# Block 2 of a two-block layer stack: selection pairs ahead of sliding pairs, window keys and values made later, latent norms in three steps

## What is computed

```
h = rmsnorm(x, mix_norm)
c_q, c_kv, k_rope, n_q, n_kc, n_vc, n_ks, n_vs, n_kw, n_vw, n_gate, sb_q, sb_k, sb_v = split(h @ w_in)
# 1. latent attention, 6 heads: softmax over all earlier tokens
q  = rmsnorm(c_q, q_norm) @ w_uq ;  k, v = rmsnorm(c_kv, kv_norm) @ w_ukv ;  rope on 32 columns
# 2. three branches that share 6 query heads (2 key heads), each with its own gate
o_cmp = softmax(q . kc) vc          # kc, vc: 31 compressed blocks, made by a small gelu MLP
o_sel = softmax(q . ks, selected blocks, causal) vs   # with 8 blocks all are selected
o_win = softmax(q . kw, sliding window 512, causal) vw
o_nsa = g0 * o_cmp + g1 * o_sel + g2 * o_win
# 3. stick-breaking attention, 4 heads
a = exp(log_sigmoid(z) + suffix sums of log_sigmoid(-z)) ;  o_sb = a v
x = x + concat(o_mla, o_nsa, o_sb) @ w_out
```

## Time and profile before

| | |
|---|---|
| median of three runs | 3490.95 us (3486.69 to 3496.64) |
| the profiled execution | 3486.4 us, span 3484.6 us |
| TensorE busy | 3376.5 us, 97% of the span |
| VectorE, ScalarE, GpSimd busy | 1652.7, 1226.2, 199.2 us |
| bytes moved | 288.19 MB |

### The profile page before, as it was taken

The page is one execution under the profiler, slowest core; times in us unless marked ns, Lnnn a source line. Parts: engine busy times, 40 slices in busy tenths (PEclk is TensorE's granted clock), DMA queues, the critical chain, the costliest instruction groups (busy, mean ns, idle before and its releaser), DMA issues.

```text
span 3484.6 us, 42143 instructions
## 1 busy us (share of the span) xinstructions
PE 3376.5 (97%) x15726; PEld 2641.3 (76%) x15726; DVE 1652.7 (47%) x2158; ACT 1226.2 (35%) x1831; POOL 199.2 (6%) x247
## 2 busy tenths in 40 slices
PE   8989999999899999999998999999999999999998
PEld 6657888775688877888775688887888776678887
DVE  6755443566444335443545554434443543654433
ACT  4343122432422234222444442234222444542233
POOL 1200000011010000000002310000000001310000
PEclk9999999999999999999999999999999999999999
DMA  6213322221243222332320143333332321033331
GB/s 167 66 43 84 97 97 96 85 79 49 61 106 99 95 92 79 96 98 96 78 64 24 30 104 96 96 97 87 96 97 100 85 73 32 16 89 96 96 96 67
DMA packets 434262, 288.19 MB, mean 83 GB/s; under 512 B 44528, under 2 KB 412316, under 8 KB 433896
## 3 DMA queue, kind: packets, MB, share of 16 engines
q1 hardware_dynamic: 431272, 280.02, 27.7%
q0 software_dynamic: 2736, 4.58, 0.9%
q10 hardware_dynamic: 144, 2.10, 0.2%
HBM read 284.53 MB, written 2.13 MB: 82 GB/s over the span
## 4 chain that ended last, share of the span: by engine, by line
PE 92%; DVE 3%; ACT 3%; issue 2%; DMA 0%; SPq 0%; DVEq 0%; ACTq 0%
PE bank L1964 27%; PE bank L1966 27%; PE bank L1965 27%; PE bank L1974 2%; PE bank L2061 1%; PE bank L2107 1%; PE bank L2083 1%; PE bank L2184 1%; PE bank L2151 1%; PE bank L2448 1%; PE bank L2450 1%; PE bank L2013 1%; PE bank L2035 0%; ACT whi L927 0%; DVE G L1506 0%
## 5 line engine op out<-in xcount | busy, mean ns | idle before, releaser
L1964 PE MATMUL bank<-hh,whi 128*128 128x512 f32 x2832 | 1140.6, 403 | 36.7 <-DVE hl L1418 22.8
L1966 PE MATMUL bank<-hh,wlo 128*128 128x512 f32 x2832 | 1107.9, 391 | 0.0
L1965 PE MATMUL bank<-hl,whi 128*128 128x512 f32 x2832 | 1107.5, 391 | 0.0
L1368 DVE TENSOR_TENSOR wlo<-raw,whi 128x1024 fp32r<-128x1024 f32 (+2 forms) x534 | 642.5, 1205 | 300.6 <-ACT whi L927 285.8
L1964 PEld LDWEIGHTS bank<-hh,whi 128*128 128x128 f32 x2832 | 535.4, 189 | 184.2 <-issue 49.4
L927 ACT ACTIVATE whi<-raw 128x1024 fp32r<-128x1024 f32 (+2 forms) x534 | 546.2, 1034 | 255.2 <-PE bank L1966 254.8
L1965 PEld LDWEIGHTS bank<-hl,whi 128*128 128x128 f32 x2832 | 535.3, 189 | 121.3 <-issue 14.2
L1966 PEld LDWEIGHTS bank<-hh,wlo 128*128 128x128 f32 x2832 | 534.5, 189 | 113.1
L1964 PE MATMUL bank<-fshi,whi 128*128 128x512 f32 (+1 forms) x1358 | 526.6, 388 | 3.5 <-DVE G L1643 2.0
L1966 PE MATMUL bank<-fshi,wlo 128*128 128x512 f32 (+1 forms) x1358 | 523.2, 385 | 0.0
L1965 PE MATMUL bank<-fslo,whi 128*128 128x512 f32 (+1 forms) x1358 | 522.8, 385 | 0.0
(11 more groups left out here) (244 smaller groups left out, 2391.6 us busy)
## 6 DMA issues: line engine op xcount, KB each, us to landing
raw<-in_ffn_w_gate SPq DMA_DIRECT2D x88, 512.0 KB, 3.8
raw<-in_ffn_w_up SPq DMA_DIRECT2D x88, 512.0 KB, 3.8
raw<-in_ffn_w_down SPq DMA_DIRECT2D x88, 512.0 KB, 3.4
raw<-in_w_in SPq DMA_DIRECT2D x78, 512.0 KB, 3.9
raw<-in_w_up SPq DMA_DIRECT2D x64, 512.0 KB, 4.0
raw<-in_w_down SPq DMA_DIRECT2D x64, 512.0 KB, 3.4
raw<-in_w_out SPq DMA_DIRECT2D x16, 512.0 KB, 4.0
raw<-in_w_in SPq DMA_DIRECT2D x18, 256.0 KB, 3.6
```

The source lines that it names most:

```text
L1368: dve.tensor_tensor(slot3(wlo, s, m), slot3(raw, s, m), slot3(whi, s, m).bitcast(F32), ALU.subtract).then_inc(c.lo_done.sem, 1)
L1964: pe.matmul(o, wh, ah, start=start, stop=False)
L1965: pe.matmul(o, wh, al, start=False, stop=False)
L1966: return pe.matmul(o, wl, ah, start=False, stop=stop)
```

## The change

It has three parts, all in block 2's mixing stage.

1. In each tile of pair entries all four sel entries come first, then the four win entries.
2. The keys and values of the win branch are made later. The full group nkw leaves `fill` and takes the place of nvwf behind `cmp_max`; the swap snkw, the full group nvwf and the transposes nvw become late groups (bank 7) and are woven with the first four pair steps. `fill` has two steps less.
3. The norm of the latents is split: `rn` is now only the sum and the reciprocal root; `rn_scale` (VectorE scaling) and `rn_split` (ScalarE high, VectorE low parts) are steps of their own, a pair step or more behind.

```diff
--- before.py
+++ after.py
@@ -197,8 +197,8 @@
     entries = []
     for t in range(NSA_PAIRS):
         entries.append(dict(kind="cmp", turn=t, t=t, new=True, done=False))
-        for i in range(QT):
-            for kind in ("sel", "win"):
+        for kind in ("sel", "win"):
+            for i in range(QT):
                 entries.append(dict(kind=kind, turn=t, t=t, i=i, n=P * (i + 1), first=False, new=False, done=kind == "win" and i == QT - 1))
     for p in range(MLA_H // 2):
         for i in range(QT):
@@ -377,8 +377,7 @@
     fill += compress(1)
     fill.append(add("gatesf", "fm", ("w_gates_pe", 0), frees="act", dst=M_POSX))
     fill += [("g", "w21"), ("g", "snks")]
-    fill.append(add("nkw", "fm", ("w_in", 1312), frees="act", dst=N_KW))
-    fill += [("g", "gates"), ("g", "snkw")]
+    fill.append(("g", "gates"))
 
     stick_steps = []
     n_stick = SB_H // 2 * QT
@@ -400,15 +399,18 @@
     steps.append(add_turned("nvs", 1184, N_TURN[0], frees="dve", dst=N_VS, off=0, pitch=128))
     steps.append(("cmp_s",))
     steps.append(("cmp_max",))
-    steps.append(add_turned("nvw", 1440, N_TURN[1], frees="dve", dst=N_VW, off=0, pitch=128))
-    steps += [("cmp_sum",), ("g", "nvs"), ("g", "nvw")]
+    steps.append(add("nkw", "fm", ("w_in", 1312), frees="act", dst=N_KW))
+    steps += [("cmp_sum",), ("g", "nvs")]
 
     late = dict(late=True)
+    groups["snkw"].update(late)
+    window = [("g", "snkw"), add_turned("nvw", 1440, N_TURN[1], frees="dve", dst=N_VW, off=0, pitch=128, **late), ("g", "nvw")]
+    groups["nvwf"].update(late)
     latent = [add(f"cq{t}", "fm", ("w_in", 128) if t else ("w_in_halves", 0), frees="act", dst=M_CQ + S * t, **late) for t in range(2)]
     latent.append(("sq", "cq"))
     latent.append(add("ckv", "fm", ("w_in", 256), frees="act", dst=M_CQ + 2 * S, **late))
-    latent += [("rn", "cq"), ("sq", "ckv")]
-    latent += [("mix", 0), ("mix", 1), ("rn", "ckv"), ("key_pe",)]
+    latent += [("rn", "cq"), ("sq", "ckv"), ("rn_scale", "cq"), ("mix", 0), ("rn_split", "cq"), ("mix", 1)]
+    latent += [("rn", "ckv"), ("key_pe",), ("rn_scale", "ckv"), ("rn_split", "ckv")]
 
     def query(h):
         if h % 3 == 0:
@@ -446,7 +448,8 @@
                 some.append(("mix", 2 + entries[k]["turn"]))
             some.append(("pair", j))
         return some
-    steps += weave(latent, run(0, O_LAG + 8))
+    steps += weave(window, run(0, QT))
+    steps += weave(latent, run(QT, O_LAG + 8))
     steps += weave(first_pair + second_pair, run(O_LAG + 8, n_nsa))
     steps += weave(third_pair, run(n_nsa, n_nsa + 6))
     steps += weave(early, run(n_nsa + 6, len(entries) + O_LAG + 1))
@@ -1279,9 +1282,11 @@
                         square(c, l, A2_KV, 0, g(M_CQ + 2 * S), narrow)
                     elif s[0] == "rn" and s[1] == "cq":
                         rms(c, l, 3, A2_Q, 2, bank[:, 7, :], 256, narrow)
+                    elif s[0] == "rn_split" and s[1] == "cq":
                         highs(c, l, 8, [fshi[:, 0, :], fshi[:, 1, :]], narrow)
                     elif s[0] == "rn":
                         rms(c, l, 4, A2_KV, 1, bank[:, 7, :], 128, narrow)
+                    elif s[0] == "rn_split":
                         highs(c, l, 10, [fshi[:, 2, :]], narrow)
                     elif s[0] == "pair":
                         pair(c, l, s[1])
@@ -1393,6 +1398,22 @@
                         dve.tensor_tensor(lo_tiles[t - 1], tmp[(t - 1) % 2], hi_tiles[t - 1].bitcast(F32), ALU.subtract).then_inc(c.rn_lo.sem, 1)
                     if beside:
                         beside(t)
+
+            def latent_scale(c, l, r, b0, at, gain, n):
+
+                _, rstd, tmp = narrow
+                dve.wait_ge(c.rn_rstd.sem, c.rn_rstd.at(l, r))
+                dve.wait_ge(c.rn_lo.sem, c.rn_lo.at(l, b0))
+                for t in range(n):
+                    dve.scalar_tensor_tensor(out=tmp[t], in0=g(at + S * t), scalar=prm[:, gain + t:gain + t + 1], in1=rstd, op0=ALU.mult,
+                                             op1=ALU.mult).then_inc(c.rn_tmp.sem, 1)
+
+            def latent_low(c, l, b0, first, n):
+
+                tmp = narrow[2]
+                for t in range(n):
+                    dve.wait_ge(c.rn_hi.sem, c.rn_hi.at(l, b0 + t + 1))
+                    dve.tensor_tensor(fslo[:, first + t, :], tmp[t], fshi[:, first + t, :].bitcast(F32), ALU.subtract).then_inc(c.rn_lo.sem, 1)
 
             def add_squares(c, l, at, t):
 
@@ -1880,10 +1901,12 @@
                         group(c, b, l, b["groups"][s[1]])
                     elif s[0] == "px":
                         blocks(c, b, l, s[1])
-                    elif s[0] == "rn" and s[1] == "cq":
-                        norm(c, l, 3, 24, [g(M_CQ), g(M_CQ + S)], prm[:, P2_QN:P2_QN + 2], [fshi[:, 0, :], fshi[:, 1, :]], [fslo[:, 0, :], fslo[:, 1, :]], narrow)
-                    elif s[0] == "rn":
-                        norm(c, l, 4, 26, [g(M_CQ + 2 * S)], prm[:, P2_KVN:P2_KVN + 1], [fshi[:, 2, :]], [fslo[:, 2, :]], narrow)
+                    elif s[0] == "rn_scale" and s[1] == "cq":
+                        latent_scale(c, l, 3, 24, M_CQ, P2_QN, 2)
+                    elif s[0] == "rn_scale":
+                        latent_scale(c, l, 4, 26, M_CQ + 2 * S, P2_KVN, 1)
+                    elif s[0] == "rn_split":
+                        latent_low(c, l, *((24, 0, 2) if s[1] == "cq" else (26, 2, 1)))
                     elif s[0] == "key_pe":
                         key_pe(c, b, l)
                     elif s[0] == "turn_q":
@@ -2043,6 +2066,8 @@
                     q, n, at, sb_ = e["q"], e["n"], P * e["i"], score_banks(e)
                     if q == 0:
                         need(c, b, l, *(gr["name"] for gr in b["order"] if gr.get("evac", True) and not gr.get("late")))
+                    if e["kind"] == "win" and e["i"] == e["t"] == 0:
+                        need(c, b, l, "snkw", "nvw")
                     if e["kind"] == "mla" and e["i"] == 0:
                         p = e["pair"]
                         need(c, b, l, f"mk{p}", *(f"mv{t}" for t in range(QT)))
```

## The result

The changed kernel takes 3504.52 us, the median of five runs (3499.69 to 3505.05), against 3486.69 us for the kernel before in the same comparison. The ratio is 1.0036, with a 95% interval of 1.0025 to 1.0048: slower. (The quotient of those two medians alone is 1.0051. The recorded ratio is smaller, and the two profiled executions side with it.) The profiled execution took 3499.69 us; its span is 3497.9 us, 13.3 us (0.38%) more than before, where 14.2 were forecast.

The account below looks back on a forecast made before the run. TensorE was taken to bound the kernel. Per layer 8.3 us (stick phase) - 2.2 (opening) + 1 (clock) = 7.1, +14.2 for two layers on 3490.95: 3505 us predicted, 8 in 10 within 3491 to 3520.

Parts of the forecast that it names:

- The new order of the fillers: Stick phase: with nkw and snkw out of `fill`, TensorE waits 12.4 us in place of 4.1, 8.3 more per layer.
- the first `sbo`: Stick phase: with c01 instead of nq2 ahead of it, it waits 4.1 us for `suf_exp 3` on ScalarE.
- `z 6`: Stick phase: waits 5.6 us for `suf_exp 4`, a 7.1 us chain with only `suf 4` and snq2 left as cover.
- The opening: Opening of the pairs: waits of 5.4 us in place of 7.6, so 2.2 us less per layer.
- The 1.4 us before nvwf: Opening: nvwf needs bank 7 and waits 1.4 us for the swap's VectorE operations, behind 0.7 of scores.
- The 1.0 before the first scores: Opening: scores of sel 0.0, without cq0 as cover, wait 1.0 us for the copy of nvs.
- The 2.7 us that I laid to `rn_scale`: Opening: VectorE's scaling delays win 0.3's scores by 0.3 us, win 0.1's transposes by 1.9, win 0.2's by 0.5.
- The clock: Stick phase and opening: lower clock behind two new waits, less one that goes, 1 us each: net +1 per layer.
- B: Opening loses its added waits and runs at clock 1.00, stick phase +8.3 without clock loss: 3484 us; chance 0.05.
- C: Two new stalls stand; opening regains half its lower-clock time, waits 2 us fewer: 3495 us; chance 0.26.
- D: Opening: six groups in a row on one bank wait for evacuations, 0.8 us more each for five: 3517 us; chance 0.13.
- E: Stick phase: the new stalls aren't there, since ScalarE or VectorE run ahead: 3483 us; chance 0.04.

Follow-up runs that it names:

- part 1 alone: Kernel before with sel entries ahead of win entries in the pairs, everything else as before: ratio 0.9986, 3482.4 us.
- Part 3 alone: Kernel before with the latent norms split into three steps, pair order and window keys untouched: ratio 0.9961, 3473.4 us.
- parts 1 and 3: Kernel before with sel entries first and the latent norms split, window keys and values where they were: ratio 0.9972, 3480.2 us.

## Why the prediction was right

The time was met (3504.5 for 3505) and so was the cause. That the time is met to half a microsecond is luck: I built on a median of 3490.95 for the kernel before, which in the comparison became 3486.69, and single executions of either kernel differ by 5 to 12 us. What can be held against the sum is the rise: 14.2 us forecast, 13.3 by the profiled spans, 12.6 by the ratio. By the steps:

- The new order of the fillers makes two long waits. At the first `sbo` 4.1 us were worked out and 3.81 measured; at `z 6` 5.6 and 5.80. The waits at `suf 1` and `z 3`, 2.0 together, became 2.06; `suf 5` went; `sbo 1` has 0.25 for 0.3. Only `z 4` was off, 1.00 for 0.4. The sum was 12.4 us; it is 12.9. The exchange of nks and `z 6` shows that the larger one costs 0.36%, nq2 ahead of `sbo` that the other costs as much; parts 1 and 2 with the norm in one step show that they come from part 2, part 1 alone having none of them.
- The opening. 5.4 us of waits were worked out, 4.8 measured. The 1.4 us before nvwf is 1.56. The 1.0 before the first scores didn't come: nkw ran its first nine matmuls at 1.2 GHz and took 7.2 us instead of the 5.6 of nvwf in its place before, so the copy of nvs was in time. A loss by the clock took the place of a wait.
- The 2.7 us that I laid to `rn_scale` (three waits, of 0.3, 1.9 and 0.5) came as two waits of 1.31 and 1.63, 2.9 together, and VectorE is what is late, as I had it. The step in between was wrong, and the match of the sums is partly luck. I had the larger ones behind GpSimd's scaling, which waits for the reciprocal. They end with VectorE's copies of transposes, as these rows of VectorE in the changed kernel show:

```profile
1882.29 1.41 DVE L1408 SCALAR_TENSOR_TENSOR G<-G,prm 128x512 f32<-128x512 f32 x2
1883.62 1.21 DVE L1517 TENSOR_REDUCE stat<-bank 128x2 f32<-128x1024 f32 x1
1884.76 0.15 DVE L1521 RECIPROCAL stat<-stat 128x2 f32<-128x2 f32 x1
1884.83 1.20 DVE L1527 COPY G<-bank 128x1024 f32<-128x1024 f32 x1
...
1892.62 0.68 DVE L1604 TENSOR_TENSOR G<-G 32x512 f32<-32x512 f32 x1
1893.34 0.69 DVE L1517 TENSOR_REDUCE stat<-bank 128x2 f32<-128x512 f32 x1
1893.95 0.95 DVE L1527 COPY G<-bank 128x768 f32<-128x768 f32 x1
```

  The copy L1527 ends at 1886.03 behind the scaling L1408 and at 1894.90 behind the last rotary operation of the keys (`key_pe`, L1604). TensorE's next transposes start at 1886.08 and 1894.95. So only the first of the two lies behind `rn_scale`; the second lies behind `key_pe`, which the forecast didn't price.
- The clock. +1 us per layer was taken. What the waits leave of the measured 7.0 and 6.3 us is 1.0 and 0.3: the waits rose by 8.8 in the stick phase and fell by 2.8 in the opening. By the windows, what the clock can have cost in layer 0 went from 10.6 us (0.05 of 106.7 and 0.08 of 66.2) to 12.1 (0.09 of 112.3 and 0.03 of 67.7). In layer 1 it hardly moved, from 13.9 to 13.5; the windows of the kernel before for it are

```profile
2797.00:2910.80 113.80, 109.64 (x538) 81.32 (x536) 45.69 (x64) 51.19 (x69) 0.00 (x0) 0.91 0.26 63
2910.80:2972.20 61.40, 53.57 (x334) 35.66 (x333) 32.57 (x55) 27.00 (x69) 12.47 (x19) 0.94 0.10 24
```

  The net was small because two terms cancelled: in layer 0 the stick phase lost 4.8 us by the clock (10.1 for 5.3) and the opening won 3.3 (2.0 for 5.3), in layer 1 it was 1.3 and 1.7. My sum had 2 us of loss behind the two new waits and 1 us of return for the one that goes; in layer 0 both were larger than that, in layer 1 the return larger and the loss smaller. So the term has the right size by cancelling, not by its parts, though the bounds I gave held both. Part 3 alone showed how much that term can be: I expected 2 to 3 us per layer and it gave 6 to 7.

Against the rivals: B (the opening gives all back) fell: the stick phase cost 8.8 us of waits and a clock loss besides, and the opening saved about 6 us in layer 0 and 4.5 in layer 1, less than the 8.3 from which B decides. C was right in its own mechanism: the opening got back 3.3 and 1.7 us of lower-clock time, where C had 2.6 and 1.6. What kept the time from C's was that the stick phase lost about as much by the clock (4.8 and 1.3), and that the waits of the opening were only 0.6 us fewer than I found, not 2. The chain D feared exists in one place only, the 1.56 us before nvwf; another order of two steps moves it to nvw and makes it 1.26. E fell with the waits of 3.81 and 5.80 us.

## What to carry to other kernels

A step taken out of a list that is woven evenly moves every other step of it; go through the new list for each latency that a moved step had covered, not only for the step that you meant to move. Where one engine is busy for 97%, price a wait by what stands behind it too: the waits of 2.7 to 5.8 us here were followed by up to twice the time for the next work, and taking away the norm's wait gave back more than its length (7.0 us for 2.0 in layer 0). Measure the parts of a change one by one: here one part alone gained 0.4% while the whole lost 0.36%, and one exchange of two steps made up for it.

## What the runs showed of the hardware

The granted clock of the opening followed neither the sum of TensorE's waits nor the longest one. In layer 0, up to mq0: with 9.0 us of waits (the longest 2.7) it was 0.90, with 7.6 (3.0) 0.92, with parts 1 and 3 6.0 (2.2) 0.95, with part 3 alone 5.6 (1.9) 1.00; but the changed kernel has only 4.8 (1.6) and 0.97. The same wait can stand before either level: with part 3 alone eight transposes behind a wait of 1.84 us took 1.09 us in layer 0 and 1.97 in layer 1.

In the changed kernel TensorE ran `z 6` and the first part of nks at 1.2 GHz behind 5.8 us of idle time (four 64x384 matmuls 1.65 us, where the earlier trace rows have 0.92), and the first `sbo` took 4.54 us for 2.37 behind 3.8 us of idle time and the narrow matmuls of c01. Idle time isn't the only thing that stands before a fall: `suf 3`, at 1759 us, ran at the lower level too (2.02 us for two 128x512, then 1.29 for the same two), behind only 1.0 us of idle time and the 24 narrow matmuls of c00, and before the change the same happened with no wait at all, behind those of c00 and c01 (2.05 us). That the narrow matmuls are the cause was not tested, and they don't bring a fall each time: behind the same 48 matmuls of 64x32 of `cmp_s`, nkw's first nine ran at the lower level in the changed kernel (7.2 us for the group) and nvwf at the full one in the kernel before (5.6 us). Trainium2's clock gate is described in the Trainium skill, page "TensorE: Matmul & The Clock Gate", part 1, as following how busy the array has been; these rows agree with it as far as idle time or narrow work stands before each of these falls.
